# Down-projection weights as runs of two neighbouring rows, and H transposed by even and odd columns

## The chip, the cores and the metric

The kernel runs on one core of a Trainium2 chip. The other cores are idle. The metric is the device time of one execution in microseconds, from the slowest (here the only) core. The engines that matter here are TensorE (PE in the profile, with its weight loads listed apart as PEld), VectorE (DVE), ScalarE (ACT), GpSimd (POOL) and SyncE (SP), which issues nearly all the large DMAs. TensorE multiplies a stationary operand, loaded by LDWEIGHTS, with a moving operand that streams through it.

## The reference, cut to what matters

Two blocks of two layers each run one after the other on 256 tokens of width 1024, all in float32. The four feed-forward parts are what the change touches. One is dense, one is a mixture of 8 experts with the two best taken, and two are mixtures of 16 experts in 4 groups. All have the same core, with different widths between up and down projection (2816 for the dense layer and the first mixture, 512 for the others).

```python
D_MODEL = 1024; D_FF = 2816; D_FF_EXPERT = 2816; D_EXPERT = D_MODEL // 2

def swiglu(u, w1, w3, w2):                      # dense, layer 0 of the first block
    return (jax.nn.silu(u @ w1) * (u @ w3)) @ w2

def run_block(args):                            # first mixture: 8 experts, width 2816
    tok_idx, e = args
    xb = tokens[tok_idx]
    return (jax.nn.silu(xb @ w1[e]) * (xb @ w3[e])) @ w2[e]

for e in range(N_EXPERTS_2):                    # the two later mixtures: 16 experts, width 512
    h = jax.nn.silu(xt @ w_gate[e]) * (xt @ w_up[e])
    out = out + combine[:, e:e + 1] * (h @ w_down[e])
```

The product `h @ w_down` sums over the hidden index. Any order of that index gives the same sum, as long as h and the rows of the down weights are taken in the same order.

## The kernel before, in words

The hidden width is cut into blocks of FSTEP = 256. For each block and expert the kernel needs 256 columns of w1 and 256 of w3 (1024 KB each, in rows of 1 KB), and 256 rows of w2 (1024 KB, in rows of 4 KB). SP loads the first two into a slot of `ring` and the third into the same slot of `dring`, a view of `dreg`. Both have RING = 4 slots. There are 11 such blocks in the dense layer, 88 in the first mixture and 32 in each of the other two.

In a slot of `dring`, partition p holds two rows of w2. Before the change these are rows p and 128 + p of the block (lines 461, 489 and 519), each a run of 4 KB in memory.

The order of DMAs in a mixture is written out in `expert_loads`: `up(i)` issues the two up loads of block i, and then `down(i - LAG)` issues the down load of the block three before. An up load waits until TensorE has used the slot's previous up weights (`moe_upped`), a down load until it has used the previous down weights (`moe_down_done`). All these DMAs go through one queue in this order.

TensorE works in rounds. In a round `up(r)` (line 1037) takes four pieces of 32 slots of tokens, which sit side by side in the four column groups of the array, against w1 and w3 (64 matmul instructions). A block has three such pieces, so four blocks make three rounds. ScalarE takes silu of one half of the result (line 1575), VectorE multiplies with the other (lines 2246, 2251) and writes H, 128 rows by 256 hidden columns. In the round behind it TensorE transposes H in two pieces of 128 columns (`turn_hidden`, line 1049), ScalarE copies the transposed pieces to HQ (line 1581), and a round later `down(i)` (line 1065) multiplies them with `dring`: piece j of HQ with row group j of the slot. A round carries one or two such downs (24 instructions each). Some rounds carry a part of the scatter of a finished bin as well (line 1097) or the transposes of its places (line 1087).

```python
for j in range(2):
    mm = pe.transpose(banks[2][:, (2 * (r % 2) + j) * P:(2 * (r % 2) + j + 1) * P],
                      H[:, r % 2, j * P:(j + 1) * P], ident[:, :])
```

In such a transpose H is the stationary operand, read by LDWEIGHTS, and the identity is the moving one. The profile names the moving operand first (bank<-ident,H).

The dense layer does the same with whole rows of 128 tokens: up at line 966, transposes of H at line 986, down at line 977. Lines 519 and 1148 belong to a second pass for bins that overflow. The trace has no instruction of it.

Of the kernel before, what the change touches and what calls it, by code (L numbers as in the profile page):

```python
# [7 lines left out]
P = 128  # L8
# [177 lines left out]
def two_blocks(nc, A, out):  # L186
# [3 lines left out]
    with ExitStack() as ctx:  # L190
        def sb(name, shape, dt=F32):
            return ctx.enter_context(nc.sbuf_tensor(name, shape, dt))
# [3 lines left out]
        def sem(name):  # L196

            if name not in sems:
                sems[name] = ctx.enter_context(nc.semaphore(name))
            return sems[name]  # L200
# [12 lines left out]
        ident = sb("ident", [P, P])  # L213
# [34 lines left out]
        SG = sb("SG", [P, 2, FSTEP])  # L248
        H = sb("H", [P, 2, FSTEP])
        HT = sb("HT", [P, 2, 2, P])  # L250

        dring = carve(dreg, 0, RING, 2, D)
        kT = carve(dreg, 0, 4, 2 * T)
# [157 lines left out]
        def _(sp):  # L411
# [34 lines left out]
            def dense_loads(w1, w3, w2):  # L446


                for st in range(NSTEP):
                    s = st % RING  # L450
                    f = slice(st * FSTEP, (st + 1) * FSTEP)
                    if st < RING:
                        slot_free(s)
                    else:
                        sp.wait_ge(sem("upped"), TT * (st - RING + 1))
                    for i, w in enumerate((w1, w3)):
                        sp.dma_start(ring[:, s, :, i * FSTEP:(i + 1) * FSTEP],
                                     w.rearrange("(k p) n -> p k n", p=P)[:, :, f]).then_inc(sem(f"pair_in{s}"), 16)
                    if st >= RING:
                        sp.wait_ge(sem("down_done"), TT * (st - RING + 1))  # L460
                    sp.dma_start(dring[:, s, :, :], w2[f, :].rearrange("(j p) n -> p j n", p=P)).then_inc(sem(f"down_in{s}"), 16)
                for st in range(NSTEP):
                    holder[st % RING] = ("upped", TT * (st + 1))

            def expert_loads(m, w1, w3, w2, updated):


                def columns(i):
                    b, q = divmod(i, m.steps)
                    e, st = divmod(q, m.halves)  # L470
                    return b * m.experts + e, slice(st * FSTEP, (st + 1) * FSTEP)

                def up(i):
                    s = i % RING
                    e, f = columns(i)
                    if i < RING:
                        slot_free(s)
                    else:
                        sp.wait_ge(sem("moe_upped"), m.before["upped"] + m.done_in(i - RING) + 1)
                    for h, w in enumerate((w1, w3)):  # L480
                        sp.dma_start(ring[:, s, :, h * FSTEP:(h + 1) * FSTEP],
                                     w(e).rearrange("(k p) n -> p k n", p=P)[:, :, f]).then_inc(sem(f"moe_up_in{s}"), 16)

                def down(i):
                    s = i % RING
                    e, f = columns(i)
                    if i >= RING:
                        sp.wait_ge(sem("moe_down_done"), m.before["down_done"] + i - RING + 1)
                    sp.dma_start(dring[:, s, :, :], w2(e)[f, :].rearrange("(j p) n -> p j n", p=P)).then_inc(
                        sem(f"moe_down_in{s}"), 16)  # L490

                for i in range(RING):
                    up(i)
                sp.wait_ge(sem("x_updated"), updated)
                for i in range(RING):
                    down(i)
                for i in range(RING, m.blocks):
                    up(i)
                    if i - LAG >= RING:
                        down(i - LAG)  # L500
                for i in range(m.blocks - LAG, m.blocks):
                    down(i)
                for s in range(RING):
                    holder[s] = ("moe_upped", m.before["upped"] + m.rounds)

            def second_loads(m, w1, w3, w2):

                with sp.If(spilled(sp, m) > 0):
                    with sp.Fori(0, m.bins) as b:
                        for r in range(2):  # L510
                            with sp.Fori(0, m.steps // unrolled(m)) as c:
                                for h in range(unrolled(m)):
                                    f = bass.ds(c * FSTEP, FSTEP) if m is MOE1 else slice(h * FSTEP, (h + 1) * FSTEP)
                                    sp.wait_ge(sem(f"baton{m.name}"), baton_at(m, b, r, c, h))
                                    for i, w in enumerate((w1, w3)):
                                        sp.dma_start(ring[:, 0, :, i * FSTEP:(i + 1) * FSTEP],
                                                     w(b, c).rearrange("(k p) n -> p k n", p=P)[:, :, f]).then_inc(
                                            sem(f"second_in{m.name}"), 16)
                                    sp.dma_start(dring[:, 0, :, :], w2(b, c)[f, :].rearrange("(j p) n -> p j n", p=P)).then_inc(
                                        sem(f"second_in{m.name}"), 16)  # L520
                    sp.wait_ge(sem(f"baton{m.name}"), 1 + 2 * m.bins * baton_bin(m))

# [146 lines left out]
        def _(pe):  # L669
# [159 lines left out]
            for t in range(TT):  # L829
                m = tok_unit(f"mo{t}", T1, t, w)  # L830
# [121 lines left out]
            def dense_ffn():  # L952


                nu = TT * NSTEP
                for i in range(nu + 2):
                    if i < nu:
                        st, t = divmod(i, TT)
                        s = st % RING
                        if t == 0:  # L960
                            pe.wait_ge(sem(f"pair_in{s}"), 32 * (st // RING + 1))
                        if i >= 2:
                            pe.wait_ge(sem("hidden"), i - 1)
                        for k in range(KC):
                            operand_chunk(k, i == 0)
                            m = pe.matmul(banks[t][:, :], T1[:, k, t * P:(t + 1) * P], ring[:, s, k, :],  # L966
                                          start=k == 0, stop=k == KC - 1)
                        m.then_inc(sem("upped"), 1)
                    if i >= 2:
                        st, t = divmod(i - 2, TT)  # L970
                        s = st % RING
                        if t == 0:
                            pe.wait_ge(sem(f"down_in{s}"), 16 * (st // RING + 1))
                        pe.wait_ge(sem("hidden_turned"), i - 1)
                        for j in range(2):
                            for n in range(2):
                                m = pe.matmul(banks[4 + 2 * t + n][:, :], HT[:, t, j, :], dring[:, s, j, n * NCH:(n + 1) * NCH],  # L977
                                              start=st == 0 and j == 0, stop=st == NSTEP - 1 and j == 1)
                        m.then_inc(sem("down_done"), 1)
                    if 1 <= i <= nu:  # L980
                        t = (i - 1) % TT
                        pe.wait_ge(sem("hidden"), i)
                        if i >= 3:
                            pe.wait_ge(sem("hidden_turned"), i - 2)
                        for j in range(2):
                            m = pe.transpose(banks[2 + t][:, j * P:(j + 1) * P], H[:, t, j * P:(j + 1) * P], ident[:, :])
                        m.then_inc(sem("turned_h"), 1)


            def moe(m, src):  # L990
# [50 lines left out]
                def turn_hidden(r):  # L1041

                    upto("hidden", r + 1)
                    if r:
                        upto("hidden_turned", r)
                    if r == 0 and m is not MOE1:
                        upto("slot_gates_taken", 1)
                    for j in range(2):
                        mm = pe.transpose(banks[2][:, (2 * (r % 2) + j) * P:(2 * (r % 2) + j + 1) * P],  # L1049
                                          H[:, r % 2, j * P:(j + 1) * P], ident[:, :])  # L1050
                    mm.then_inc(sem("moe_turned_h"), 1)

                def down(i):
# [91 lines left out]

                def turn_again(b, r, c, h):
                    for j in range(2):
                        i = pe.transpose(banks[5][:, j * P:(j + 1) * P], H[:, 0, j * P:(j + 1) * P], ident[:, :])
                    return i

                def down_again(b, r, c, h):
# [1309 lines left out]
```

## Time and profile before

| | before |
|---|---|
| median of 3 runs | 2666.06 us |
| lowest and highest | 2664.68 and 2666.22 us |
| the profiled execution | 2663.96 us |
| its span in the profile | 2662.2 us |
| mean granted TensorE clock | 0.931 of full |
| TensorE matmul busy | 2386.3 us, 90% |
| data moved | 644.52 MB, mean 242 GB/s |

The span runs from the first to the last instruction; 1.8 us of the profiled execution lie outside it. The profile lists busy time per engine and, for each group of instructions, what ended the engine's idle time before it. Matmuls overlap in the pipeline, so the start of one group to the start of the next is a better measure than the lengths shown. A DMA share above 1 means that packets of one engine overlap in time.

### The profile page before, as it was taken

How to read it: one execution, taken by the hardware profiler on the slowest of the kernel's cores; microseconds unless marked ns; L12 is line 12 of the kernel's file. 1: busy time of each engine (PE TensorE's matmuls, PEld its weight loads, DVE VectorE, ACT ScalarE, POOL GpSimd, SP SyncE). 2: the span in 40 equal slices, each digit the busy share in tenths (PEclk: the TensorE clock that was granted, in tenths of full speed). 3: DMA queues.
4: the chain of work that ended last, by engine and by line, in shares of the span. 5: the costliest groups of instructions: out<-in, count | busy, mean ns of one | idle time of the engine just before them, and what ended most of it. 6: DMA issues, size and time to landing. Idle time of an engine off the chain costs nothing. (4 is left out here: it accounts for less than half of the span.)

```text
span 2662.2 us, 34403 instructions
## 1 busy us (share of the span) xinstructions
PE 2386.3 (90%) x15188; PEld 1033.9 (39%) x15188; DVE 512.7 (19%) x1140; ACT 335.2 (13%) x781; POOL 85.9 (3%) x139
## 2 busy tenths in 40 slices
PE   4997877999884689999999999987799998789997
PEld 2573653444663343222222222244422227442222
DVE  2033342000269410000000000013200012210002
ACT  2013221000210220000000000011100010210000
POOL 2000000000034000000000000000000000000000
PEclk9998678999997889999999999988799999879999
DMA  8222146542562459999999999940799982359994
GB/s 279 95 95 95 64 169 213 193 151 79 190 252 95 161 177 336 351 366 364 367 365 365 365 365 365 320 165 2 259 351 366 362 319 88 97 197 362 364 361 154
DMA packets 446101, 644.52 MB, mean 242 GB/s; under 512 B 10723, under 2 KB 345019, under 8 KB 445947
## 3 DMA queue, kind: packets, MB, share of 16 engines
q1 hardware_dynamic: 442011, 629.55, 68.9%
q0 software_dynamic: 3936, 12.69, 1.5%
q8 instruction: 125, 2.05, 0.3%
q14 instruction: 29, 0.24, 0.0%
HBM read 641.15 MB, written 1.05 MB: 241 GB/s over the span
## 5 line engine op out<-in xcount | busy, mean ns | idle before, releaser
L1037 PE MATMUL bank<-ring,wide 128*32 128x512 f32 x7296 | 809.7, 596 | 2.4 <-issue 1.5
L1037 PEld LDWEIGHTS bank<-ring,wide 128*32 128x32 f32 x7296 | 232.1, 110 | 550.6 <-issue 550.5
L1065 PE MATMUL bank<-dreg,RB 128*32 128x512 f32 x3648 | 415.0, 595 | 0.0
L1575 ACT ACTIVATE SG<-bank 128x256 f32<-128x256 f32 x114 | 43.7, 383 | 1194.5 <-PE bank L1037 1194.5
L1065 PEld LDWEIGHTS bank<-dreg,RB 128*32 128x32 f32 x3648 | 106.8, 109 | 223.8 <-issue 223.8
L709 PE MATMUL bank<-wide,ring 128*128 128x256 f32 x832 | 182.8, 382 | 6.6 <-DVE wide L1863 6.6
L699 PE MATMUL bank<-ring,wide 128*128 128x512 f32 x416 | 182.1, 598 | 0.0
L709 PEld LDWEIGHTS bank<-wide,ring 128*128 128x128 f32 x832 | 159.3, 192 | 29.8 <-issue 8.1
L2246 DVE TENSOR_TENSOR H<-SG,bank 128x256 f32<-128x256 f32 x66 | 27.8, 421 | 722.9 <-ACT SG L1575 722.9
L966 PE MATMUL bank<-ring,wide 128*128 128x512 f32 x352 | 157.2, 600 | 6.4 <-DMA ring<-in_l_ffn_w 6.4
L699 PEld LDWEIGHTS bank<-ring,wide 128*128 128x128 f32 x416 | 79.8, 193 | 97.2 <-issue 97.0
L2150 DVE SCALAR_TENSOR_TENSOR T<-dreg,PCOL,T 128x256 f32<-128x256 f32 x210 | 103.9, 572 | 0.1
L966 PEld LDWEIGHTS bank<-ring,wide 128*128 128x128 f32 x352 | 66.2, 193 | 82.5 <-issue 82.5
L699 PE MATMUL bank<-ring,T 128*128 128x512 f32 x192 | 84.7, 601 | 1.6 <-ACT sm L1714 0.9
L2251 DVE SCALAR_TENSOR_TENSOR H<-SG,sgt,bank 128x256 f32<-128x256 f32 x32 | 15.4, 481 | 341.5 <-ACT SG L1575 341.5
L977 PE MATMUL bank<-dreg,HT 128*128 128x512 f32 x176 | 79.3, 593 | 1.0 <-ACT HT L1528 1.0
L720 PE MATMUL bank<-ring,CB 128*32 128x512 f32 x384 | 56.4, 725 | 23.1 <-DMA ring<-in_l_mod_w 23.0
L1097 PE MATMUL bank<-T 128*128 128x512 f32 x128 | 69.5, 636 | 3.9 <-ACT T L1592 3.9
L1049 PEld LDWEIGHTS bank<-ident,H 128*128 128x128 f32 x228 | 23.1, 140 | 95.0 <-issue 95.0
L699 PEld LDWEIGHTS bank<-ring,T 128*128 128x128 f32 x192 | 36.9, 193 | 48.0 <-issue 45.8
L2107 DVE TENSOR_TENSOR H<-SG,bank 128x256 f32<-128x256 f32 x22 | 9.3, 421 | 223.4 <-ACT SG L1521 223.4
L2270 DVE TENSOR_TENSOR TOK<-bank,TOK 128x512 f32<-128x512 f32 x64 | 43.9, 686 | 41.6 <-PE bank L1097 41.6
(369 smaller groups left out, 1466.8 us busy)
## 6 DMA issues: line engine op xcount, KB each, us to landing
ring<-in_l_moe_w SPq DMA_DIRECT2D x176, 1024.0 KB, 11.5
dreg<-in_l_moe_w SPq DMA_DIRECT2D x88, 1024.0 KB, 12.2
ring<-in_w_gate SPq DMA_DIRECT2D x64, 1024.0 KB, 11.3
ring<-in_w_up SPq DMA_DIRECT2D x64, 1024.0 KB, 13.5
dreg<-in_w_down SPq DMA_DIRECT2D x64, 1024.0 KB, 12.3
ring<-in_l_mod_w SPq DMA_DIRECT2D x24, 2048.0 KB, 8.0
ring<-in_l_ffn_w SPq DMA_DIRECT2D x22, 1024.0 KB, 10.3
ring<-in_l_w_in SPq DMA_DIRECT2D x7, 2048.0 KB, 7.8
```

The lines of the kernel that those rows point to most:

```text
L699: m = pe.matmul(o[:, lo:lo + n], src[:, k, t * P:(t + 1) * P], w[:, k, 0:n], start=k == 0, stop=k == KC - 1)
L709: m = pe.matmul(o[:, i * T:(i + 1) * T], w[:, k, (2 * j + i) * P:(2 * j + i + 1) * P], src[:, k, :], start=k == 0, stop=k == KC - 1)
L720: m = pe.matmul(o[QUAD * g:QUAD * (g + 1), :], CQ[:, 4 * r + g, :], w[:, 4 * r + g, :], start=r == 0, stop=r == 1)
L966: m = pe.matmul(banks[t][:, :], T1[:, k, t * P:(t + 1) * P], ring[:, s, k, :], start=k == 0, stop=k == KC - 1)
L977: m = pe.matmul(banks[4 + 2 * t + n][:, :], HT[:, t, j, :], dring[:, s, j, n * NCH:(n + 1) * NCH], start=st == 0 and j == 0, stop=st == NS ...
L1037: mm = pe.matmul(banks[r % 2][32 * g:32 * g + 32, :], xg[:, k, at:at + 32], ring[:, i % RING, k, :], start=k == 0, stop=k == KC - 1)
L1065: return pe.matmul(banks[4 + 2 * (b % 2) + h][32 * g:32 * g + 32, :], HQ[:, r % 4, j, 32 * q:32 * q + 32], dring[:, i % RING, j, h * NCH:( ...
L1097: pe.matmul(o[:, :], PTM[:, 2 * h + t, :], YS[:, h * NCH:(h + 1) * NCH], start=True, stop=True).then_inc(sem("moe_scattered"), 1)
L1575: act.activation(SG[:, r % 2, :], banks[r % 2][:, 0:FSTEP], ACT.Silu).then_inc(sem("moe_silued"), 1)
L2150: dve.scalar_tensor_tensor(T2[:, k, :], hT[:, k, tap:tap + T], w, T2[:, k, :], ALU.mult, ALU.add).then_inc(sem("tap"), 1)
L2246: i = dve.tensor_tensor(H[:, r % 2, :], SG[:, r % 2, :], banks[r % 2][:, FSTEP:NCH], ALU.mult)
L2270: dve.tensor_tensor(v, o[:, :], v, ALU.add).then_inc(sem("moe_added"), 1)
```

## The change

The load of a down block now gives partition p the rows 2p and 2p + 1 of the block. They are neighbours in memory, so a partition's part is one run of 8 KB and no longer two of 4 KB. Source and destination of each such DMA change in the program from 128x2x1024 to 128x2048 elements. Row group j of a slot then holds the rows 2p + j. For the sum to match, the transposes take the columns 2n + j of H, in a view `HI`: their LDWEIGHTS reads every second float32 of a row of H.

No instruction is added, removed or moved on any engine. Copies, matmuls, semaphores and the order of the DMAs are as they were.

```diff
--- before.py
+++ after.py
@@ -248,6 +248,7 @@
         SG = sb("SG", [P, 2, FSTEP])
         H = sb("H", [P, 2, FSTEP])
         HT = sb("HT", [P, 2, 2, P])
+        HI = H[:, :, :].rearrange("p q (n j) -> p q j n", j=2)
 
         dring = carve(dreg, 0, RING, 2, D)
         kT = carve(dreg, 0, 4, 2 * T)
@@ -458,7 +459,7 @@
                                      w.rearrange("(k p) n -> p k n", p=P)[:, :, f]).then_inc(sem(f"pair_in{s}"), 16)
                     if st >= RING:
                         sp.wait_ge(sem("down_done"), TT * (st - RING + 1))
-                    sp.dma_start(dring[:, s, :, :], w2[f, :].rearrange("(j p) n -> p j n", p=P)).then_inc(sem(f"down_in{s}"), 16)
+                    sp.dma_start(dring[:, s, :, :], w2[f, :].rearrange("(p j) n -> p j n", j=2)).then_inc(sem(f"down_in{s}"), 16)
                 for st in range(NSTEP):
                     holder[st % RING] = ("upped", TT * (st + 1))
 
@@ -486,7 +487,7 @@
                     e, f = columns(i)
                     if i >= RING:
                         sp.wait_ge(sem("moe_down_done"), m.before["down_done"] + i - RING + 1)
-                    sp.dma_start(dring[:, s, :, :], w2(e)[f, :].rearrange("(j p) n -> p j n", p=P)).then_inc(
+                    sp.dma_start(dring[:, s, :, :], w2(e)[f, :].rearrange("(p j) n -> p j n", j=2)).then_inc(
                         sem(f"moe_down_in{s}"), 16)
 
                 for i in range(RING):
@@ -516,7 +517,7 @@
                                         sp.dma_start(ring[:, 0, :, i * FSTEP:(i + 1) * FSTEP],
                                                      w(b, c).rearrange("(k p) n -> p k n", p=P)[:, :, f]).then_inc(
                                             sem(f"second_in{m.name}"), 16)
-                                    sp.dma_start(dring[:, 0, :, :], w2(b, c)[f, :].rearrange("(j p) n -> p j n", p=P)).then_inc(
+                                    sp.dma_start(dring[:, 0, :, :], w2(b, c)[f, :].rearrange("(p j) n -> p j n", j=2)).then_inc(
                                         sem(f"second_in{m.name}"), 16)
                     sp.wait_ge(sem(f"baton{m.name}"), 1 + 2 * m.bins * baton_bin(m))
 
@@ -983,7 +984,7 @@
                         if i >= 3:
                             pe.wait_ge(sem("hidden_turned"), i - 2)
                         for j in range(2):
-                            m = pe.transpose(banks[2 + t][:, j * P:(j + 1) * P], H[:, t, j * P:(j + 1) * P], ident[:, :])
+                            m = pe.transpose(banks[2 + t][:, j * P:(j + 1) * P], HI[:, t, j, :], ident[:, :])
                         m.then_inc(sem("turned_h"), 1)
 
 
@@ -1047,7 +1048,7 @@
                         upto("slot_gates_taken", 1)
                     for j in range(2):
                         mm = pe.transpose(banks[2][:, (2 * (r % 2) + j) * P:(2 * (r % 2) + j + 1) * P],
-                                          H[:, r % 2, j * P:(j + 1) * P], ident[:, :])
+                                          HI[:, r % 2, j, :], ident[:, :])
                     mm.then_inc(sem("moe_turned_h"), 1)
 
                 def down(i):
@@ -1145,7 +1146,7 @@
 
                 def turn_again(b, r, c, h):
                     for j in range(2):
-                        i = pe.transpose(banks[5][:, j * P:(j + 1) * P], H[:, 0, j * P:(j + 1) * P], ident[:, :])
+                        i = pe.transpose(banks[5][:, j * P:(j + 1) * P], HI[:, 0, j, :], ident[:, :])
                     return i
 
                 def down_again(b, r, c, h):
```

## Rows read from the trace of the kernel before

**Rows 1.** The profile's page: the span, and DMA share in 40 slices.

```profile
span 2662.2 us, 34403 instructions
DMA  8222146542562459999999999940799982359994
```

**Rows 2.** Stretches: us, busy of PE, PEld, DVE, ACT, POOL, PEclk, DMA share, GB/s.

```profile
1100.00:1700.00 600.00, 598.65 (x5178) 176.14 (x5178) 41.48 (x91) 48.56 (x127) 0.00 (x0) 1.00 1.07 365
```

**Rows 3.** The page's groups: count | busy us, mean ns | idle before, releaser.

```profile
L1037 PE MATMUL bank<-ring,wide 128*32 128x512 f32 x7296 | 809.7, 596 | 2.4 <-issue 1.5
...
L1065 PE MATMUL bank<-dreg,RB 128*32 128x512 f32 x3648 | 415.0, 595 | 0.0
```

**Rows 4.** Timeline of PE, first mixture: start us, us, what (1240 to 1312).

```profile
1243.14 7.07 PE L1037 MATMUL bank<-ring,wide 128*32 128x512 f32 x64
...
1253.11 7.05 PE L1037 MATMUL bank<-ring,wide 128*32 128x512 f32 x64
...
1265.63 7.05 PE L1037 MATMUL bank<-ring,wide 128*32 128x512 f32 x64
...
1276.28 7.07 PE L1037 MATMUL bank<-ring,wide 128*32 128x512 f32 x64
...
1299.94 7.08 PE L1037 MATMUL bank<-ring,wide 128*32 128x512 f32 x64
...
1311.08 7.07 PE L1037 MATMUL bank<-ring,wide 128*32 128x512 f32 x64
```

**Rows 5.** The same view at three later rounds; in brackets idle time before.

```profile
1472.28 7.07 PE L1037 MATMUL bank<-ring,wide 128*32 128x512 f32 x64
...
1483.16 3.21 PE L1037 MATMUL bank<-ring,wide 128*32 128x512 f32 x28 [0.73 <-issue]
...
1645.67 7.05 PE L1037 MATMUL bank<-ring,wide 128*32 128x512 f32 x64
...
1656.97 3.59 PE L1037 MATMUL bank<-ring,wide 128*32 128x512 f32 x29 [0.58 <-issue]
...
1991.20 7.07 PE L1037 MATMUL bank<-ring,wide 128*32 128x512 f32 x64
...
2001.54 1.92 PE L1037 MATMUL bank<-ring,wide 128*32 128x512 f32 x16 [0.18 <-issue]
```

**Rows 6.** Waits of SP's queue: us in total, times, longest.

```profile
SPq L481 <- PE bank L1037: 301.4, 54, 39.7
...
SPq L489 <- PE bank L1065: 162.6, 67, 10.8
```

**Rows 7.** Stretches with up loads alone, then down loads alone (columns of rows 2).

```profile
925.00:938.00 13.00, 5.93 (x29) 5.93 (x29) 10.81 (x19) 4.17 (x10) 0.23 (x2) 0.59 1.10 352
939.50:948.50 9.00, 3.35 (x17) 3.28 (x17) 3.10 (x15) 1.77 (x3) 0.00 (x0) 0.50 0.91 361
```

**Rows 8.** DMA issues: count, KB each, median us from issue to landing.

```profile
dreg<-in_l_moe_w SPq DMA_DIRECT2D x88, 1024.0 KB, 12.2
...
dreg<-in_w_down SPq DMA_DIRECT2D x64, 1024.0 KB, 12.3
...
dreg<-in_l_ffn_w SPq DMA_DIRECT2D x11, 1024.0 KB, 5.2
```

**Rows 9.** Timeline of all engines around one pair of transposes.

```profile
1214.14 0.20 PEld L1049 LDWEIGHTS bank<-ident,H 128*128 128x128 f32 x2 [0.84 <-issue]
1214.14 0.44 PE L1049 MATMUL bank<-ident,H 128*128 128x128 f32 x2
...
1214.51 0.14 PEld L1065 LDWEIGHTS bank<-dreg,RB 128*32 128x32 f32 x6 [0.17 <-issue]
```

**Rows 10.** Weight loads of lines 1049 and 986: ns min/median/max, first and last start.

```profile
L1049 PEld LDWEIGHTS bank<-ident,H x228: 137/141/143, 982.5 to 2631.7; 128*128 128x128 f32 x114
...
L986 PEld LDWEIGHTS bank<-ident,H x44: 139/141/143, 460.2 to 675.5; 128*128 128x128 f32 x44
```

## The prediction

> **What bounds the kernel now.** I read the span and the slices first. The kernel takes 2662.2 us, and the DMA digit is 9 in the stretches of the three mixtures [rows 1]. So the question is whether TensorE or the DMAs set the pace there, since the change makes one class of DMA different. In the stretch from 1100 to 1700 us, inside the first mixture, TensorE is busy for 598.65 of 600 us at full clock, and the DMAs move 365 GB/s at a share of 1.07 [rows 2]. Both look full. The page's groups decide which one waits: the up matmuls of line 1037 had 2.4 us of idle time before them in the whole program, and the down matmuls of line 1065, which read the weights whose layout changes, had 0.0 [rows 3]. No down matmul waits for its weights.
>
> The timeline gives TensorE's own need. A round with one down takes 1253.11 - 1243.14 = 9.97 us, one with two downs 1265.63 - 1253.11 = 12.52, one with the transposes of the places 1276.28 - 1265.63 = 10.65, so 0.68 more, and one with a scatter 1311.08 - 1299.94 = 11.14, so 1.17 more [rows 4]. A bin of the first mixture has 11 blocks, 8.25 rounds, 11 downs, four scatters and one set of places: 8.25 x 9.97 + 2.75 x 2.55 + 4 x 1.17 + 0.68 = 94.6 us, or 8.60 us per block. A block is three DMAs of 1024 KB [rows 8], 3.146 MB. At 365 GB/s [rows 2] that is 8.62 us. The two are equal within the error of this sum. In the other mixtures a bin has 8 blocks and 6 rounds: 6 x 9.97 + 2 x 2.55 + 4 x 1.17 + 0.68 = 70.3, or 8.79 us per block, so there TensorE is slower than the DMAs by 0.17 us a block.
>
> That balance shows in two more places. SP waited for TensorE to free slots, 301.4 us before up loads and 162.6 us before down loads [rows 6], as it does when DMAs run ahead. And TensorE does lose time to late up weights in a few rounds, which the view files under "issue". The round from 1472.28 lasts 10.88 us where 9.97 is normal, the one from 1645.67 lasts 11.30 where 10.65 is normal, the one from 1991.20 lasts 10.34 where 9.97 is normal [rows 5]. That is 0.91 + 0.65 + 0.37 = 1.93 us. Their marked idle time, 0.73 + 0.58 + 0.18, is the 1.5 us of issue in [rows 3]; it is a little shorter than the delay, since the ends of matmuls are modelled.
>
> **The change, part by part.** *The DMAs.* 88 + 64 + 11 = 163 loads [rows 8] go from 256 runs of 4 KB to 128 runs of 8 KB. The trace has no load with 8 KB runs, so I bound it from the nearest two. With up loads alone (runs of 1 KB) the DMAs move 352 GB/s at a share of 1.10, so 320 GB/s per full share. With down loads alone (4 KB) they move 361 at 0.91, so 397 [rows 7]. Over 16 engines that is 51.2 ns for a 1 KB run and 165.1 ns for a 4 KB run. A straight line through both gives 13.2 ns per run and 38.0 ns per KB, hence 317 ns for 8 KB against 330 for two of 4 KB. An engine has 8 such runs in a load of 1024 KB, so a down load costs 2.54 us and not 2.64, a gain of 0.10 us per block. The far end on the good side is the line's per-run term gone twice over, 0.2 us. The far end on the bad side is the rate of the 1 KB runs, 3.28 us, so 0.64 worse. I take the gain of 0.10, since the three points 1, 4 and 8 KB should lie on one line.
>
> What that gain is worth is read from TensorE. The block's DMA time goes from 8.62 to 8.52 us, below TensorE's 8.60. All that can come back is the 1.93 us of late rounds; everything else lies under matmuls that run back to back. In the dense layer a load lands 5.2 us after its issue [rows 8], which says that the queue is mostly empty there, and its downs don't appear among the waiting groups. I count nothing for it. Sum: -1.9 us.
>
> The Trainium skill, "Perfetto Trace Analysis", section "DMA Optimizations", says that larger DMAs use the memory's bandwidth better and that going from 2 KB to 4 or 8 KB can improve throughput dramatically. By this rule the DMA-full mixtures should shorten; that is the first rival below. The trace disagrees as to its worth: the engine that would profit has 1.35 us of idle time in 600.
>
> *The weight loads of the transposes.* 228 + 44 = 272 loads of H [rows 10] read every second element. Each takes 141 ns [rows 10]. Around one pair, both together last 0.20 us, so the second starts 0.06 us behind the first, and from the first transpose to the first down matmul 0.37 us pass [rows 9]. The loads stand on TensorE's path there: the engine that sets the end does nothing else in these 0.37 us. No PE operand in the program before is read with a step of two, so the trace shows no price. The lower bound is zero, since a wider step can't make a read faster. If the read goes at half speed, each load holds the engine 0.06 us longer: 272 x 0.06 = 16.3 us. If the whole of a load doubles, 272 x 0.14 = 38 us. I take zero, by the nearest rows, loads of the same 128 columns whose size and count do not change, and keep 16.3 us as a rival.
>
> The Trainium skill, "SBUF — State Buffer", section "Door 1: The DMA port swizzle", has a note on cachelines. It states that reads run at full rate as long as at least two fall into a line of 16 bytes, and names up to four float32. A step of two float32 gives exactly two per line. By this the price is zero; by a rule that every skipped word costs, it would be the 16.3 us. No run so far shows which.
>
> *The rest.* ScalarE's copies, VectorE's products and all down matmuls read and write what they did, in the same shape. SP issues the same number of DMAs in the same order. If an issue gets shorter, SP only waits longer for a free slot [rows 6]. If down loads land 0.10 us earlier, they free nothing for TensorE, and the up loads behind them in the queue land earlier by as much, which is what removes the late rounds.
>
> Sum: 2663.96 - 1.9 = 2662.1 us for the profiled execution. The median of the runs stands 2.1 us above the profiled execution, so 2664.2 us for the median.
>
> **The rivals.**
>
> *The mixtures are bound by the DMAs (faster).* The flat 365 GB/s over 600 us speaks for it [rows 2], and the equality of 8.62 and 8.60 us. If TensorE's blocks were only as long as the DMAs let them be, 0.10 us per block would come back in 88 + 64 = 152 blocks: -15 us, 2651 us. Against it: rounds of one kind have one length, 9.97 us, whether or not weights landed early, and idle time before line 1065 is 0.0 [rows 3, 4]. A round bound by transfers would vary.
>
> *The stepped weight load goes at half speed (slower).* Place: between up and down of each of the 136 rounds or units, on TensorE. Price: 0.06 us x 272 = +16.3, less the 1.9 of late rounds, since a slower TensorE waits for no weights: about +14, 2680 us. It decides as soon as a load costs more than 0.02 us extra (5.4 us in all). For it: 0.06 us for 128 columns is already close to one column per cycle of 2.4 GHz, so any loss of read rate shows at once. Against it: nothing in the trace.
>
> *The 8 KB runs move more slowly (slower).* Fewer and longer runs per engine, with other addresses open at a time. Here the balance of 8.62 and 8.60 makes the first mixture pay for everything: if a down load takes 5% longer (0.13 us), 79 blocks behind the start pay it, +10 us, while the others hide it in their 0.17 us: 2676 us. At the bad end of 0.64 us it is 79 x 0.62 + 56 x 0.47 = +75 us, 2741 us. It decides from 0.07 us per load (79 x 0.07 = 5.5 us). For it: the first mixture has no slack. Against it: rate rises with the run from 1 to 4 KB [rows 7].
>
> *The change doesn't do what it says*: the DMA hardware cuts 8 KB runs into pieces of 4 KB, so that the loads are as before. Then nothing changes, 2666 us. It has the same sign as the forecast.
>
> **How the numbers follow.** The forecast has 0.65, the case of the same packets 0.13, DMA-bound mixtures 0.07, the stepped load 0.08, slower 8 KB runs 0.07. What a measurement of this kernel can tell from no change is about 0.2%, 5.3 us. The forecast and the unchanged packets both lie within it, and 0.02 of them are left for straying out, half on each side. So faster 0.08, same 0.76, slower 0.16. The range runs from 2661 us (the forecast less 3 us for spread and for small waits that I left out) to 2676 us, which takes in slower runs up to 5%. Left out are the half-speed weight load, the DMA-bound mixtures and the worse half of the slower runs, 0.08 + 0.07 + 0.03 = 0.18. The likeliest case's own range is 2661 to 2668.
>
> **What would show it.** In the profile after, the DMAs' packets should be fewer by 163 x 128, some 21,000, in all, and the DMA share of the stretch 1100 to 1700 should sink below 1.07 at the same 365 GB/s, since TensorE sets the rate. SP's waits for TensorE should grow. The idle time before line 1037 should fall from 2.4 to about 1 us, and the bracketed waits should be gone. The weight loads of lines 1049 and 986 should stay at 141 ns and the pair at 0.37 us. The forecast is wrong if rounds of one down take less than 9.9 us or more than 10.05 us, if idle time appears before lines 1037 or 1065, or if the packets' count is unchanged.

## The result, and the profile after

| | before | after |
|---|---|---|
| median of 14 runs each | 2665.77 us | 2672.41 us |
| lowest and highest | 2659.75 and 2668.84 us | 2669.48 and 2674.65 us |
| the profiled execution's span | 2662.2 us | 2670.9 us |

The change made the kernel slower: ratio 1.0025 with a 95% interval of 1.0017 to 1.0033. That is +6.6 us where I had forecast -1.9. The time of 2672.41 us lies inside the range of 2661 to 2676, but the change has the other sign, and it is just past the 0.2% for which I gave "slower" a chance of 0.16.

The page after, its rows of the span, packets, queue and groups. Columns of the groups: count, busy us, mean ns, idle before.

```profile
span 2670.9 us, 34403 instructions
...
DMA packets 425237, 644.52 MB, mean 241 GB/s; under 512 B 10723, under 2 KB 345019, under 8 KB 404219
...
q1 hardware_dynamic: 421147, 629.55, 68.0%
...
L1038 PE MATMUL bank<-ring,wide 128*32 128x512 f32 x7296 | 810.3, 596 | 0.9 <-ACT wide L1569 0.9
...
L1066 PE MATMUL bank<-dreg,RB 128*32 128x512 f32 x3648 | 415.0, 595 | 0.0
```

The DMAs did what was forecast. There are 425237 packets, 20864 = 163 x 128 fewer than the 446101 of before, so the 8 KB runs are not cut. Their queue takes 68.0% of the engines' span and not 68.9%: 0.680 x 2670.9 = 1816 us against 0.689 x 2662.2 = 1834, so 18 us over 163 loads, 0.11 us per load. I had 0.10. The idle time by "issue" before the up matmuls, 1.5 us in [rows 3], is gone. The line numbers are one higher than before.

The stretch of [rows 2] after: TensorE has no idle time at all, at the same 365 GB/s and a share of 1.06.

```profile
1100.00:1700.00 600.00, 600.00 (x5168) 179.92 (x5164) 40.78 (x89) 50.11 (x125) 0.00 (x0) 1.00 1.06 365
```

The weight loads of H after (ns min/median/max, first and last start). They were 141 ns in [rows 10]. In line 1050 the median stands at the lower edge, since the second load of a pair takes longer than the first; the mean there is 206 ns and was 140.

```profile
L1050 PEld LDWEIGHTS bank<-ident,H x228: 194/196/223, 983.6 to 2640.4; 128*128 128x128 f32 x114
...
L987 PEld LDWEIGHTS bank<-ident,H x44: 194/196/200, 461.6 to 677.1; 128*128 128x128 f32 x44
```

And the timeline of TensorE after, the rounds that answer to [rows 4].

```profile
1245.69 7.07 PE L1038 MATMUL bank<-ring,wide 128*32 128x512 f32 x64
1252.70 0.50 PE L1050 MATMUL bank<-ident,H 128*128 128x128 f32 x2
1253.13 2.78 PE L1066 MATMUL bank<-dreg,RB 128*32 128x512 f32 x24
1255.73 7.05 PE L1038 MATMUL bank<-ring,wide 128*32 128x512 f32 x64
...
1268.32 7.05 PE L1038 MATMUL bank<-ring,wide 128*32 128x512 f32 x64
...
1279.03 3.21 PE L1038 MATMUL bank<-ring,wide 128*32 128x512 f32 x28
```

A round with one down takes 10.04 us (9.97 in [rows 4]), one with two downs 12.59 (12.52), one with the places 10.71 (10.65). From the first transpose to the first down matmul there are now 0.43 us and not 0.37. The loss is 0.06 to 0.07 us in each round. Over the 114 rounds of the mixtures this is some 7.4 us (at 0.065).

### The profile page after: what moved, and what is told of

Read it like the earlier page. It is cut to its first block and busy times, and to the rows that moved or that the text cites. A ratio compares the mean times of both kernels' runs of the same rounds, so it can differ in the third digit from the quotient of the medians.

```text
span 2670.9 us, 34403 instructions
## 1 busy us (share of the span) xinstructions
PE 2394.3 (90%) x15188; PEld 1047.1 (39%) x15188; DVE 512.4 (19%) x1140; ACT 340.0 (13%) x781; POOL 85.8 (3%) x139
## 2 busy tenths in 40 slices
DMA packets 425237, 644.52 MB, mean 241 GB/s; under 512 B 10723, under 2 KB 345019, under 8 KB 404219
## 5 line engine op out<-in xcount | busy, mean ns | idle before, releaser
L1050 PEld LDWEIGHTS bank<-ident,H 128*128 128x128 f32 x228 | 36.1, 206 | 94.8 <-issue 94.8
L1050 PE MATMUL bank<-ident,H 128*128 128x128 f32 x228 | 57.3, 333 | 0.0
```

## The experiments

Each group of stretches below has the first mixture from its third round to its last, then the stage from there to the second mixture, then the second mixture from its third round to its last, then the stage to the third mixture. The columns are those of [rows 2]: the stretch, its length, the busy time of five engines with their instructions, the granted clock of TensorE, the DMA share and GB/s. Some groups show only the first two or three of these stretches. "Stage" below means the part between two mixtures. The same for before:

```profile
985.51:1716.63 731.12, 729.77 (x6283) 215.48 (x6282) 47.29 (x104) 59.72 (x154) 0.00 (x0) 1.00 1.05 357
1716.63:1909.16 192.53, 147.77 (x599) 87.54 (x599) 46.26 (x110) 34.13 (x78) 5.58 (x9) 0.83 0.42 148
1945.57:2167.07 221.50, 221.31 (x1915) 64.84 (x1907) 16.11 (x34) 18.20 (x47) 0.00 (x0) 1.00 1.04 356
2167.07:2363.20 196.13, 155.54 (x704) 106.37 (x703) 48.42 (x109) 30.76 (x72) 1.15 (x3) 0.87 0.40 142
```

### The runs alone

```diff
 (the changed kernel)
-HI[:, r % 2, j, :]
+H[:, r % 2, j * P:(j + 1) * P]          # and likewise in the dense layer and the second pass
```

> The 8 KB runs of the change, with H transposed as before in two blocks of 128 neighbouring columns (the rows of w2 and of H then don't belong together, so the product is another one). Theory A (the stepped weight load is the whole loss, the runs give back the late rounds): weight loads of H at 141 ns, a round with one down back at 9.95 us, no idle time of line 1038 by issue, and the median 2 us below before, ratio 0.999. Rival B (the 8 KB runs are the loss): ratio 1.002 or more. Rival C (nothing but scatter of the runs): ratio 1.000, and the same for the kernel with the step alone.

Measured: 2666.96 us against 2665.33 in the same series, ratio 1.0009 (1.0000 to 1.0018). Weight loads are at 141 ns again, and the idle time by issue is gone.

```profile
986.22:1715.22 729.00, 729.00 (x6284) 213.84 (x6283) 47.29 (x104) 59.77 (x154) 0.00 (x0) 1.00 1.04 358
1715.22:1909.72 194.50, 150.04 (x599) 89.25 (x598) 46.24 (x110) 34.27 (x78) 5.58 (x9) 0.82 0.41 146
1946.21:2167.31 221.10, 221.10 (x1914) 64.53 (x1906) 16.11 (x34) 18.22 (x47) 0.00 (x0) 1.00 1.03 357
```

The first mixture is 2.12 us shorter than before, the second 0.40. This is the gain that I had forecast, 1.9 us, and a little more. But the stage behind the first mixture is 1.97 us longer, and the median shows no gain. Rival B is out: the runs don't cost the 5 us and more that it needs. Theory A holds for the mixtures and misses the total. The last experiments follow this up.

### The step alone

```diff
 (the changed kernel)
-w2(e)[f, :].rearrange("(p j) n -> p j n", j=2)
+w2(e)[f, :].rearrange("(j p) n -> p j n", p=P)   # in all three loads of w2
```

> The loads of 4 KB runs as before, with H transposed by even and odd columns (the product is another one). Theory A: weight loads of H at 196 ns, each round of the mixtures 0.067 us longer, 114 x 0.067 = 7.6 us, plus 0.2 in the dense layer, less some of the late rounds, since a slower TensorE waits for fewer weights: ratio 1.002 to 1.003. Rival B: ratio 1.000. If the late rounds hide the step partly, it will be near 1.002.

Measured: 2671.99 us, ratio 1.0035 (1.0021 to 1.0048). This ratio is not the quotient of the two medians, which is 1.0025.

```profile
984.62:1718.30 733.68, 733.44 (x6284) 221.94 (x6283) 47.29 (x104) 62.50 (x154) 0.00 (x0) 1.00 1.05 356
1718.30:1905.84 187.54, 142.95 (x600) 84.11 (x599) 46.25 (x110) 34.16 (x78) 5.58 (x9) 0.86 0.43 152
```

The first mixture takes 733.68 us and the second 222.41, so 2.6 and 0.9 more than before. The late rounds are gone here as well, with the old runs, all but 0.4 us (733.68 against the 733.24 of the changed kernel): TensorE has become slow enough for the DMAs. So the step is the loss, whatever the runs, and rival C, mere scatter, is out.

### VectorE sorts

```diff
 (the changed kernel; H transposed by neighbouring columns)
-dve.tensor_tensor(H[:, r % 2, :], SG[:, r % 2, :], banks[r % 2][:, FSTEP:NCH], ALU.mult)
+dve.tensor_tensor(pieces(H[:, r % 2, :]), parity(SG[:, r % 2, :]), parity(banks[r % 2][:, FSTEP:NCH]), ALU.mult)
+parity = lambda v: v.rearrange("p (n j) -> p j n", j=2)
+pieces = lambda v: v.rearrange("p (j n) -> p j n", j=2)
```

> The 8 KB runs, and VectorE sorts: it reads its two inputs by even and odd columns and writes H as two blocks of 128 neighbouring columns, so that TensorE's loads have no step. Theory A: weight loads of H at 141 ns, rounds as in the kernel before; VectorE's product may take longer than 0.42 us, up to twice, but has some 10 us of idle time per round, so it costs nothing. Median 2 us below before, ratio 0.999, the fastest of the kernels. Rival: VectorE's later product delays the first or last rounds of a stage by 0.4 us each, which would be too little to see; if the ratio is 1.002 like the change, the step was not the cause.

Measured: 2665.91 us, ratio 1.0007 (0.9998 to 1.0016). VectorE's product with stepped inputs, in the page's groups of this kernel:

```profile
L2248 DVE TENSOR_TENSOR H<-SG,bank 128x256 f32<-128x256 f32 x66 | 27.9, 422 | 720.7 <-ACT SG L1577 720.7
```

It took 421 ns before, so sorting is free there, even reading PSUM. The weight loads are back at 141 ns and the mixtures have lost the step's cost in full, with the 8 KB runs kept. Of the 2 us that were to come on top, the mixtures show all (729.00 and 221.33), the total nothing: the forecast of this run, the fastest of the kernels, was missed.

### Runs of 2 KB

```diff
 (the kernel before)
-dring = carve(dreg, 0, RING, 2, D)
+dring = carve(dreg, 0, RING, 2, 2, NCH)                         # slot, half, row, column
-sp.dma_start(dring[:, s, :, :], w2(e)[f, :].rearrange("(j p) n -> p j n", p=P))
+sp.dma_start(dring[:, s, :, :, :], w2(e)[f, :].rearrange("(j p) (h n) -> p h j n", p=P, h=2))
```

> The kernel before with the down weights in four runs of 2 KB per partition (rows p and 128 + p, each in two halves). This tests the balance that the prediction read: by the line through 1 and 4 KB runs a 2 KB run takes 89.2 ns, 32 per engine, 2.85 us per load and not 2.64. If the first mixture has no slack in its DMAs, its 79 blocks behind the start pay 0.2 us each, some 15 us, and the others 0.05: +16 us, ratio 1.006, with idle time before line 1037 of 10 us or more. If TensorE alone sets the pace and has slack, ratio 1.000.

Measured: 2673.39 us, ratio 1.0035 (1.0022 to 1.0049). The up matmuls' row of the page, and the queue's:

```profile
q1 hardware_dynamic: 483739, 629.55, 70.1%
...
L1037 PE MATMUL bank<-ring,wide 128*32 128x512 f32 x7296 | 808.7, 595 | 11.2 <-issue 10.3
```

```profile
985.97:1726.11 740.14, 730.33 (x6283) 217.75 (x6282) 47.27 (x104) 59.88 (x154) 0.00 (x0) 1.00 1.06 353
1726.11:1914.10 187.99, 143.82 (x600) 84.64 (x599) 46.26 (x110) 34.05 (x78) 5.59 (x9) 0.85 0.44 153
```

The first mixture is 9.0 us longer than before, with 9.8 us of TensorE idle in it. The second takes 221.24 us and the third 221.81, against 221.50 and 221.11 before. Its block takes 3.146 MB / 353 GB/s = 8.91 us by the rate. The queue's time is 0.701 x 2667.3 = 1870 us, 0.22 us more per load than in the kernel before, where the line through 1 and 4 KB said 0.21. So the balance was read rightly: in the first mixture a slower load is paid for at once, and a faster one brings back only the late rounds. The price was 9.0 and not 15 us, and 11.1 against the 729.00 us of a mixture without late rounds. That I let each block pay from the start, though a little slack exists, would explain it; no run shows this. The stage behind the mixture is 4.5 us shorter than before (187.99 at a clock of 0.85 against 192.53 at 0.83), though its matmuls are the same. This will matter below.

### Steps of the weight load

```diff
 (the changed kernel)
-HI[:, r % 2, j, :]
+src[:, j, 0:STEPS[r % 5] * P:STEPS[r % 5]]          # STEPS = (1, 2, 3, 4, 8)
```

> The changed kernel; in the mixtures the transposes read their stationary operand from a tile that stands still, with a step of 1, 2, 3, 4 or 8 float32 by round (r mod 5), in place of H, so the product is another one. It asks for the law of the step. If the loss is one of half rate for every line of 16 bytes that gives fewer than four values, the loads take 141, 196, about 230, 250, 250 ns or more: the time grows up to step 4 and is flat behind it. Rival: any step but 1 costs the same 196 ns. Second rival: the time grows with the step without end, 8 being above 400 ns. A pair costs the round the difference of one load or a little more.

Five rounds that follow each other, steps 8, 1, 2, 3 and 4 in this order, in the timeline of weight loads. A row is a pair of loads.

```profile
1203.31 0.30 PEld L1051 LDWEIGHTS bank<-ident,XN 128*128 128x128 f32 x2 [0.84 <-issue]
...
1214.51 0.20 PEld L1051 LDWEIGHTS bank<-ident,XN 128*128 128x128 f32 x2 [0.84 <-issue]
...
1225.65 0.31 PEld L1051 LDWEIGHTS bank<-ident,XN 128*128 128x128 f32 x2 [0.84 <-issue]
...
1239.43 0.31 PEld L1051 LDWEIGHTS bank<-ident,XN 128*128 128x128 f32 x2 [0.84 <-issue]
...
1250.63 0.32 PEld L1051 LDWEIGHTS bank<-ident,XN 128*128 128x128 f32 x2 [0.84 <-issue]
```

Only step 1 has 0.20 us a pair; 2, 3, 4 and 8 all have 0.30 to 0.32. Over the 114 pairs of the kernel the first load of a pair has a median of 138 ns with step 1 and of 185 to 196 with the other four, the second 142 and 208 to 219. It is a switch and no slope, as the first rival had it. A step of eight costs no more than one of two.

### The step on the moving side

```diff
 (the runs alone)
-ident = sb("ident", [P, P])
+IDW = sb("IDW", [P, 2 * P])
+ident = IDW[:, :].rearrange("p (n j) -> p j n", j=2)[:, 0, :]
```

> The 8 KB runs, H transposed by neighbouring columns (another product), and the identity, the moving operand of every transpose, spread over twice the width and read with a step of two float32. If the price of a step lies in reading SBUF as such, the transposes' matmuls, 273 ns at the least, grow by some 55 ns per 128 columns and a round by 0.1 us. If it lies in the weight load alone, the moving side shows nothing: loads 141 ns, round with one down 9.95 us. I expect the second less than the first, 0.4 to 0.6.

The groups of this kernel (count, busy us, mean ns, idle before):

```profile
L1051 PE MATMUL bank<-IDW,H 128*128 128x128 f32 x228 | 50.8, 304 | 0.0
L1051 PEld LDWEIGHTS bank<-IDW,H 128*128 128x128 f32 x228 | 23.1, 140 | 94.9 <-issue 94.9
```

The pairs' matmuls are busy for 50.8 us where they were 49.8 in the kernel before and 57.3 in the changed one. A stepped moving operand costs 1 us over 228 transposes, a stepped stationary one 7.5. The price sits in the weight load. The one execution took 2661.94 us, against 2666.90 of the kernel before beside it, though the transposes had become slower. Its first mixture takes 729.75 us and the stage behind it 188.12. That called for a look at the stages.

### Both kernels once more

> The kernel before, for a second profile. Theory D: the 2 us that the 8 KB runs save in the first mixture are lost in the stage behind it, since TensorE's granted clock falls and rises there at other instructions; a kernel repeats its own pattern. Then the stretch from the third round of the first mixture to the start of the second is 923.6 us again, split 731.1 + 192.5. Rival E: that stage scatters from run to run by 2 to 7 us whatever the kernel; then the second part is another number between 187 and 195.

> The changed kernel, for a second profile. Weight loads of H 196 ns, rounds with one down 10.01 us, first mixture from its third round 733.2 us and second and third 222.4 us from their third, all as in its first profile. Theory D: the stage behind the first mixture is 190.3 us again. Rival E: another number.

The kernel before, a second profile (2665.77 us), the first four stretches:

```profile
983.94:1714.79 730.85, 729.64 (x6283) 215.47 (x6282) 47.30 (x104) 59.82 (x154) 0.00 (x0) 1.00 1.05 358
1714.79:1907.55 192.76, 148.03 (x599) 87.73 (x598) 46.27 (x110) 34.15 (x78) 5.59 (x9) 0.83 0.42 148
1943.97:2165.08 221.11, 221.11 (x1914) 64.56 (x1907) 16.12 (x34) 18.22 (x47) 0.00 (x0) 1.00 1.04 357
2165.08:2364.98 199.90, 159.42 (x703) 108.53 (x703) 48.41 (x109) 30.88 (x72) 1.16 (x3) 0.85 0.39 139
```

The changed kernel, a second profile (2672.53 us); its first profile had 733.24, 190.30, 222.41 and 200.37:

```profile
986.47:1719.70 733.23, 733.23 (x6283) 220.98 (x6282) 47.30 (x104) 62.76 (x154) 0.00 (x0) 1.00 1.04 356
1719.70:1910.04 190.34, 145.74 (x600) 86.36 (x599) 46.27 (x110) 34.10 (x78) 5.58 (x9) 0.84 0.42 149
1946.64:2169.05 222.41, 222.41 (x1914) 66.72 (x1906) 16.11 (x34) 19.14 (x47) 0.00 (x0) 1.00 1.02 355
2169.05:2369.45 200.40, 159.26 (x704) 108.53 (x703) 48.41 (x109) 30.93 (x72) 1.16 (x3) 0.85 0.39 138
```

For the stage behind the first mixture rival E is out, as far as two profiles of each kernel can tell: it repeats to 0.3 us in both. The runs alone and VectorE sorts, which have the same first mixture, also have the same stage (194.50 us both). The total does scatter, in other places: the third round of the first mixture starts between 983.5 and 987.4 us in the profiles of this case, at 985.51 and 983.94 in the two of before. And mixture plus stage is nearly one number for both kernels: 731.12 + 192.53 = 923.65 and 730.85 + 192.76 = 923.61 before, 733.24 + 190.30 = 923.54 and 733.23 + 190.34 = 923.57 after. The runs alone have 729.00 + 194.50 = 923.50. So the 4.24 us that the step costs in the first mixture (733.24 less 729.00) are given back behind it. The second stage of before is 196.13 in one profile and 199.90 in the other, behind mixtures that differ by 0.39 us (the late round of [rows 5]).

### Further transposes in the first mixture

```diff
 (VectorE sorts; EXTRA = 6, 12 or 24)
-for j in range(2):
+for j in ((0, 0, 1) if m is MOE1 and 20 <= r < 20 + EXTRA else range(2)):
```

> The kernel in which VectorE sorts, with 6 further transposes (a repeat of one that is made anyway), one per round from round 20 of the first mixture. They lengthen it by 6 x 0.11 = 0.7 us and do nothing else. Theory D (the stage behind the mixture follows the instruction at which the granted clock changes): the sum of first mixture from its third round and the stage behind it is not 923.5 + 0.7 but 923.5, or another value 2 to 6 us away, and the same in every run; the kernel with the spread identity had 917.9 at a mixture of 729.8. So the median may fall to 2660 although work was added. Rival F (stages add up): 924.2, median 0.7 above the kernel in which VectorE sorts, 2666.6.

> The same with 12 further transposes, 1.3 us. Theory D: sum 923.5 or 2 to 6 us away from it, unchanged by 1.3. Rival F: 924.8, median 2667.2.

> The same with 24 further transposes, 2.6 us, which makes the first mixture 731.6 us long from its third round, between the kernel before (731.1) and the changed one (733.2). Theory D: sum 923.5 like theirs, stage 191.9 us. Rival F: sum 926.1 and stage 194.5.

First mixture and stage behind it with 0 (VectorE sorts), 6, 12 and 24 further transposes, one fence for each kernel:

```profile
983.50:1712.50 729.00, 729.00 (x6283) 214.40 (x6282) 47.31 (x104) 59.71 (x154) 0.00 (x0) 1.00 1.04 358
1712.50:1907.00 194.50, 150.06 (x599) 89.39 (x598) 46.26 (x110) 34.23 (x78) 5.59 (x9) 0.82 0.41 146
```

```profile
984.15:1713.82 729.67, 729.67 (x6290) 214.54 (x6289) 47.38 (x104) 59.95 (x154) 0.00 (x0) 1.00 1.04 358
1713.82:1907.64 193.82, 149.79 (x599) 89.07 (x599) 46.26 (x110) 34.23 (x78) 5.58 (x9) 0.82 0.41 146
```

```profile
984.24:1714.55 730.31, 730.31 (x6296) 215.17 (x6295) 47.32 (x104) 60.31 (x154) 0.00 (x0) 1.00 1.04 358
1714.55:1907.73 193.18, 148.71 (x599) 87.99 (x599) 46.27 (x110) 34.26 (x78) 5.58 (x9) 0.84 0.42 147
```

```profile
984.91:1716.53 731.62, 731.62 (x6307) 216.44 (x6306) 47.39 (x104) 60.74 (x154) 0.00 (x0) 1.00 1.04 357
1716.53:1910.86 194.33, 149.57 (x599) 89.16 (x598) 46.27 (x110) 34.23 (x78) 5.59 (x9) 0.83 0.41 146
```

The sums are 923.50, 923.49, 923.49 and 925.95 us. Work of 0.67 and of 1.31 us vanished to 0.01 us, as theory D had it, though D had left open another sum as well; with 2.62 us the sum jumped by 2.45. So the 923.5 expected for 24 was wrong. Rival F hit this one (926.1) and missed the other two. In the kernel with 24 the second stage takes 194.56 us behind a mixture of 221.10, where the kernels with 6 and 12 have 199.94 and 199.96 behind the same length. So the length of the mixture in front doesn't fix a stage by itself. The medians are 2666.05 us with 6 and 2666.77 us with 12 further transposes, ratios to the kernel before 0.9994 (0.9985 to 1.0003) and 0.9998 (0.9989 to 1.0007), where VectorE sorts without them had 1.0007: no slower than without them.

### A version from the experiments

```diff
 (VectorE sorts)
-ident = sb("ident", [P, P])
+IDW = sb("IDW", [P, 2 * P])
+ident = IDW[:, :].rearrange("p (n j) -> p j n", j=2)[:, 0, :]
```

> VectorE sorts (8 KB runs, no step in the weight loads), and the identity is read with a step of two as the moving operand of every transpose. It computes the reference's result. In rounds of the mixtures the step costs 0.01 us each, 1 us in all. Theory D: the stage behind the first mixture repeats the short pattern of the kernel with the spread identity: 729.8 + 188.1 = 917.9 us and not 923.5, and the median falls to 2661 or 2662, ratio 0.9985, although each transpose got dearer. Rival F (stages add up): ratio 1.0010, as VectorE sorts plus 1 us.

```profile
987.42:1717.17 729.75, 729.75 (x6283) 213.98 (x6282) 47.72 (x104) 60.28 (x154) 0.00 (x0) 1.00 1.04 358
1717.17:1905.27 188.10, 144.00 (x599) 84.74 (x598) 46.27 (x110) 34.07 (x78) 5.59 (x9) 0.85 0.43 151
```

Measured: 2661.87 us against 2665.51, ratio 0.9987 (0.9978 to 0.9996), as theory D had it and rival F not. It beats the kernel before by 3.6 us, and the changed one, measured in another series, by some 10. The mixture is 0.75 us longer than in VectorE sorts and the stage behind it 6.4 us shorter, 917.85 in sum, as in the first kernel with the spread identity (917.87). The gain lies in the stage behind, at a granted clock of 0.85 and not 0.82. The spread identity also changes how the transposes inside that stage read, but this isn't needed for the short stage: the 2 KB runs have it too (187.99), with the identity as it was. By the sums of the kernels with further transposes, another change in front of the stage may lose the gain.

## Why the prediction was wrong

**Where the bound is: right.** TensorE sets the pace of the mixtures and the DMAs of the first one have almost no slack. With 2 KB runs, 0.22 us more per load cost 9.0 us there; with 8 KB runs, 0.11 us less brought back 2.12, the late rounds, and no more.

**The DMAs: right.** 0.10 us per load forecast, 0.11 measured. The late rounds were worth 2.5 us (2.12 + 0.40) where I had summed 1.93. The DMA-bound rival fell, which had asked for 15. The Trainium skill, "Perfetto Trace Analysis", section "DMA Optimizations", says that going from 2 KB to 4 or 8 KB can improve throughput dramatically. Here the step from 4 to 8 KB took 0.11 us off a load of 2.64, and beyond the late rounds the time didn't fall, since TensorE was busy for 598.65 of 600 us already.

**The stepped weight load: the step that failed.** I wrote "I take zero, by the nearest rows, loads of the same 128 columns whose size and count do not change". These rows couldn't show what a step costs, and I gave the other end, 16.3 us, only 0.08. The load takes 196 ns and not 141 by the medians, 55 ns more, and 206 and not 140 by the means of the mixtures, about the 0.06 of the rival. Its mechanism was right, its price was not: I charged 272 loads in full. In a round of the mixtures only some 0.065 us for a pair reach the path, not 0.12, and in the dense layer, whose matmuls use all 128 columns of the array and take some 592 ns each, 0.2 us in all 22 units (from the first transpose to the last 215.3 us before and 215.5 after). So 7.4 + 0.2 = 7.6 us. With the 1.9 of late rounds off, that gives 5.7, against the measured 6.6. That the two are so close is partly luck, since this sum lets everything reach the total, as the next part shows. Of my signs of being wrong, a round with one down above 10.05 us would have missed this: it took 10.04. The 141 ns of the loads, which I had expected to stay, show it.

The Trainium skill, "SBUF — State Buffer", section "Door 1: The DMA port swizzle", calls reads free while at least two fall into a line of 16 bytes. A step of two float32 gives two per line and is not free for this engine's weight loads; step 8, with one per two lines, costs the same as step 2. Here the measurement decides. For the moving operand with step 2 the rule holds nearly: 1 us in 228 transposes.

**What I didn't see: the stages between the mixtures.** I added and took off microseconds as if each reached the total. Across the first mixture and the stage behind it they don't: mixtures of 729.00, 731.12 and 733.24 us all end in 923.5 to 923.65. This is no law: other kernels end in 917.85 (VectorE sorts with the spread identity), 921.22 (the step alone), 925.95 (24 further transposes) and 928.13 (2 KB runs). The stage has the same number of matmuls each time, and its length goes roughly with the granted clock: 0.82 where it takes 194.50 us, 0.83 at 192.53, 0.84 at 190.30, 0.85 at 188.10, 0.86 at 187.54; 194.33 at 0.83 and 193.18 at 0.84 are off this line. TensorE waits often there (busy for 147.77 of 192.53 us), and its clock changes between the 1.2 GHz and the 2.4 GHz level at other instructions when the mixture in front ends earlier or later. Eight transposes of that stage show it, in the kernel before and in the runs alone, each in the timeline and in the columns of [rows 2]:

```profile
1830.36 1.10 PE L1302 MATMUL bank<-ident,TOK 128*128 128x128 f32 x8 [1.42 <-DVE sm L2360]
1830.36:1831.46 1.10, 1.10 (x8) 0.86 (x8) 0.00 (x0) 0.32 (x1) 0.00 (x0) 1.00 0.00 0
...
1829.73 1.97 PE L1303 MATMUL bank<-ident,TOK 128*128 128x128 f32 x8 [1.41 <-DVE sm L2361]
1829.73:1831.70 1.97, 1.97 (x8) 1.57 (x8) 0.00 (x0) 0.60 (x1) 0.00 (x0) 0.50 0.00 0
```

The same eight take 1.10 us at a granted clock of 1.00 and 1.97 us at 0.50, behind the same wait of 1.4 us. By this reading the 2 us from the runs were turned into time at the lower level, and the 4.2 us that the step costs in the first mixture came back. Some other chain of work, begun early, that ends the stage at a fixed time would also hide them; but sums of 917.85 and 921.22, below 923.5, speak against it. Behind the second mixture the two kernels differ: mixture and stage take 417.63 and 421.01 us before, 422.78 and 422.81 after.

Between the profiles of the runs alone and of the changed kernel, which differ by the step only, the span grows by 4.6 us: 4.24 in the first mixture, 4.20 less in the stage behind it, 1.31 in each of the other two, 0.44 in the second stage, 0.89 from its end to the third round of the third mixture, and 0.6 in the rest.

The eight transposes show what the clock costs at one place. That the clock, and not a wait, makes the whole difference of a stage isn't shown: no run held the clock fixed. The split of the 6.6 us over the stages is open too: each kernel has two profiles, and before differs from itself by 3.4 us in the second mixture and the stage behind it.

**Chances and range.** The range held the time, by luck: its upper part was there for slower 8 KB runs, and they were faster. A chance of 0.08 for the stepped load was too low for an operation that the trace didn't show at all and that stands alone on the path of the engine that sets the pace.

## What to carry to other kernels

When an engine is full, look at the access patterns that a change hands to it before the transfers that it saves: here 18 us less of DMA time met a full TensorE, and about half of the 55 ns more per weight load stood on its path. If a layout must interleave, let an engine with idle time do it; VectorE did it in the pass that it made anyway, at 422 ns for 421. In a kernel whose TensorE alternates between full and waiting stages, a gain or loss of 1 to 3 us in one stage says little about the total: compare the stages one by one, and then their sums.

## What the hardware showed that I had not expected

- A weight load of 128 columns of float32 takes 141 ns with step 1 and 196 ns with step 2 (medians; the means in the mixtures are 140 and 206); a pair takes 0.20 us with step 1 and 0.30 to 0.32 us with steps 2, 3, 4 and 8 alike. The moving operand with step 2 costs nearly nothing, 1 us in 228 transposes.
- VectorE multiplies float32 with step 2 from SBUF and PSUM as fast as with step 1: 422 and 421 ns for 128x256.
- DMA runs of 2, 4 and 8 KB lie nearly on one line: 0.22 us more and 0.11 us less per load of 1024 KB than with 4 KB, where the line through 1 and 4 KB said 0.21 and 0.10.
- Up to 1.3 us of added TensorE work in one stage vanished from the sum with the next, to 0.01 us, and 0.75 us of it, in another form, came with a sum 5.6 us shorter.
- The same eight transposes took 1.10 us in one kernel and 1.97 us in another, though the programs differ only in how the down weights lie; the granted clock there was 1.00 and 0.50.
